# The activations of the feed-forward networks move into the work buffer, and the down weights by 160 bytes

## What is computed

```python
D_FF = -(-8 * D_MODEL // (3 * 256)) * 256        # 2816
def swiglu(x, w_gate, w_up, w_down):
    return (jax.nn.silu(x @ w_gate) * (x @ w_up)) @ w_down
```

## The kernel before

| tile | used as | byte in the partition | modulo 512 |
|---|---|---|---|
| `uT_h`, `uT_l` | moving (and weights in the output projections) | 32896, 41088 | 128 |
| `ring_r` | weights or moving | 63104 | 128 |
| `in_h` | weights | 49280 | 128 |
| `h_r` | weights of `down` | 112256 (over `ffb`) | 128 |
| `w_gu` | weights of `gate_up` | 138336 (start of `wk`) | 96 |
| `w_dn` | moving in `down` | 171136 | 128 |
| `out_h` (three) | moving in the output projections | 191584, 207968, 179296 | 96 |
| `fox_sum` (two), `fox_head` | moving and weights of a small product | 173152, 174176, 172128 | 96 |
| `odd_small` (two) | weights, 8 columns | 61568, 61824 | 128, 384 |

## Time and profile before

### The profile page before, as it was taken

The page is one execution under the profiler, slowest core; times in us unless marked ns, Lnnn a source line. Parts: engine busy times, 40 slices in busy tenths (PEclk is TensorE's granted clock), DMA queues, the critical chain, the costliest instruction groups (busy, mean ns, idle before and its releaser), DMA issues. The chain is left out here.

```text
span 1417.8 us, 25483 instructions
## 1 busy us (share of the span) xinstructions
PE 1390.4 (98%) x10044; PEld 1285.9 (91%) x10044; DVE 944.7 (67%) x1539; ACT 690.6 (49%) x1107; POOL 83.1 (6%) x137
## 2 busy tenths in 40 slices
PE   8999999999999999999999999999999999999997
PEld 8898888999989999899989999999998988899997
DVE  5768567666668666567567666676665676676665
ACT  6764546443354443376654443444443656643342
POOL 1030010000020000000000000100000123000000
PEclk9999999999999999999999999999999999999999
DMA  9344006655536554423356555365545423464540
GB/s 360 136 161 186 2 16 237 221 180 180 194 116 223 207 193 178 179 100 132 126 198 226 199 178 181 131 228 197 197 178 179 149 90 135 178 223 179 194 160 30
DMA packets 33069, 239.47 MB, mean 169 GB/s; under 512 B 6864, under 2 KB 13280, under 8 KB 14304
## 3 DMA queue, kind: packets, MB, share of 16 engines
q1 hardware_dynamic: 30320, 234.84, 45.6%
q10 hardware_dynamic: 2672, 3.58, 0.7%
HBM read 236.15 MB, written 2.25 MB: 168 GB/s over the span
## 5 line engine op out<-in xcount | busy, mean ns | idle before, releaser
L498 PE MATMUL ps<-uT_h,w_gu 128*128 128x256 f32 x3520 | 614.1, 280 | 2.6 <-ACT uT_h L1316 2.6
L498 PEld LDWEIGHTS ps<-uT_h,w_gu 128*128 128x128 f32 x3520 | 537.5, 188 | 13.4 <-issue 5.2
L498 PE MATMUL ps<-uT_l,w_gu 128*128 128x256 f32 x1760 | 478.9, 279 | 0.0
L498 PEld LDWEIGHTS ps<-uT_l,w_gu 128*128 128x128 f32 x1760 | 325.5, 188 | 0.0
L498 PE MATMUL ps<-w_dn,h_r 128*128 128x512 f32 x1320 | 320.9, 392 | 0.3 <-DVE h_r L2070 0.3
L1368 ACT CAST w_gu<-ring 128x2048 fp32r<-128x2048 f32 x110 | 209.8, 1908 | 153.5 <-PE ps L498 152.7
L498 PEld LDWEIGHTS ps<-w_dn,h_r 128*128 128x128 f32 x1320 | 239.7, 188 | 47.3 <-issue 1.5
L2028 DVE TENSOR_TENSOR w_gu<-ring,w_gu 128x2048 fp32r<-128x2048 f32 x110 | 252.1, 2292 | 35.2 <-ACT w_gu L1368 35.2
L2061 DVE TENSOR_TENSOR us<-ps,bc 128x256 f32<-128x256 f32 x110 | 46.5, 423 | 200.1 <-PE ps L498 200.1
L1381 ACT ACTIVATE wk<-wk 128x256 f32<-128x256 f32 x110 | 46.0, 418 | 263.8 <-DVE wk L2059 263.8
L1374 ACT CAST w_dn<-ring 128x1024 fp32r<-128x1024 f32 x110 | 115.6, 1051 | 78.4 <-PE ps L498 78.3
(11 more groups left out here) (398 smaller groups left out, 1696.1 us busy)
## 6 DMA issues: line engine op xcount, KB each, us to landing
ring<-wstream SPq DMA_DIRECT2D x144, 1536.0 KB, 6.5
cst<-consts_in SPq DMA_DIRECT2D x1, 2185.0 KB, 13.7
wk<-t_row ACTq DMA_DIRECT2D x1, 2048.0 KB, 7.8
wk<-masks_in SPq DMA_DIRECT2D x1, 1216.0 KB, 23.9
x<-x_in SPq DMA_DIRECT2D x2, 512.0 KB, 4.8
ring<-wstream SPq DMA_DIRECT2D x1, 1024.0 KB, 9.0
inh<-gains ACTq DMA_DIRECT2D x2, 512.0 KB, 9.7
tri_blocks<-wk SPq DMA_DIRECT2D x3, 256.0 KB, 2.8
```

What stands on the lines that cost most here:

```text
L498: return pe.matmul(o, l, r, start=start, stop=stop, skip_group_check=True)
```

## The change

The tile `h_r` no longer lies over `ffb`. It lies in the work buffer `wk`, right behind `w_dn`. `w_dn` starts 40 floats (160 bytes) later, and the gate results `sg` follow behind the new place of `h_r`.

```diff
-        w_dn = over("w_dn", [P, 2, 2, D], "wk", 8 * D + 8)
-        h_r = over("h_r", [P, 2, 2, T], "ffb")
+        w_dn = over("w_dn", [P, 2, 2, D], "wk", 8 * D + 48)
+        h_r = over("h_r", [P, 2, 2, T], "wk", 12 * D + 48)
...
-        sg = wk[:, 12 * D + 8:12 * D + 8 + 2 * T].rearrange("p (a b) -> p a b", a=2)
+        sg = wk[:, 13 * D + 48:13 * D + 48 + 2 * T].rearrange("p (a b) -> p a b", a=2)
```

## The result

The changed kernel takes 1425.35 us (median of 6 runs, 1424.87 to 1426.12), the one before 1420.21 us (6 runs, 1419.88 to 1420.95). The ratio is 1.0037, 95% interval 1.0027 to 1.0048: slower by 5.1 us, where 4.4 us less was forecast. The time is the one that the rival "the moving read gets dearer" gave, but the trace shows another mechanism.

What follows compares the result with a forecast made beforehand. PE was taken to bound the kernel. From 1419.59 us, down's matmuls gave -4.4 and gate_up, DVE and ACT, and order 0, so 1415.2 us; forecast's own range 1409 to 1417, 8-in-10 range 1409 to 1425.6.

Steps and rivals of the forecast that it cites:

- the moving read gets dearer: Rival: down's moving read at 288 costs 4.4 ns more per matmul, +5.8 us, 1425.4 us; chance 0.28.
- What bounds the kernel: PE, busy 98% of the span at 2.4 GHz and in all of the 8.36 us step; only its spending moves time.
- Step 1: Down's 1320 matmuls, both operands moved from 128 to 288 modulo 512: -3.3 ns each, -4.4 us.
- The bounds: Limits for down's matmuls: -15.8 us if weight reads cost nothing, +5.8 us at the dear neighbour's 234.4 ns.
- Step 2: Gate_up's matmuls, operands unmoved: cost taken as 0, with 1.1 us either way for the seams.
- the seams: Where gate_up and down meet in each step, first weights loading beside the other's last matmul; 1.1 us either way.
- Step 3: DVE and ACT work on the moved tiles: at most 0.2 us a step, hidden by over 6 us; cost 0.
- Step 4: Order and waits: all five programs keep the same waits, no queue passed, no transfer starts earlier; cost 0.
- only the difference counts: Rival: down's reads collide by their distance, 0 modulo 512 before and after; same pattern, no change, 1419.6 us; chance 0.30.
- What would show it: Trace checks: gate_up 5.60 us, down about 2.72; down 2.76 means the difference rule, 2.81 or more the dear moving read.
- The rule of the two independent read ports: Skill text against the whole change: weight loads take no read bandwidth from the running matmul, so placement is worth nothing.

Runs made afterwards that it cites:

- e6: Kernel before, but each network has its own equal remainder for w_dn and h_r (96, 160, 192, 224, 256 modulo 512), w_gu at 96; 1421.12 us.
- e1: Kernel before with h_r moved into the work buffer behind w_dn, both still at 128 modulo 512; 1420.2 us against 1420.2, ratio 1.000.
- e2: Kernel before with h_r moved into the work buffer at 288 modulo 512, w_dn left at 128; 1427.37 us, ratio 1.0049.
- e3: Kernel before with w_dn alone moved to 288 modulo 512, h_r left in its own tile at 128; 1427.53 us, ratio 1.0056.
- e4: Changed kernel plus one 64-column matmul, its result overwritten, ahead of each gate_up but a network's first; no address changed; 1432.87 us in one run.
- e13: e9 plus one 64-column matmul, its result overwritten, ahead of each gate_up but a network's first; no address changed; 1420.94 us.
- e7: Code of e6 with w_dn and h_r at 128; w_gu at 128 in networks 1 and 2, 160 in 3 and 4, 192 in 5; 1430.55 us.
- e9: Code of e6 with w_gu at 192 in all networks; w_dn and h_r as equal pairs at 96, 160, 192, 224, 256; 1416.32 us beside 1419.65 before.
- e10: As e9, with the equal pairs of w_dn and h_r at 288, 320, 352, 416, 480; 1415.66 us beside 1419.65 before.
- e11: Code of e6 with all pairs at 160; w_gu at 64 in networks 1 and 2, 256 in 3 and 4, 320 in 5; 1427.91 us.
- e12: Kernel before with w_gu at 192, w_dn and h_r at 224 modulo 512 in all networks, h_r in the work buffer; 1405.13 us against 1420.12, ratio 0.9895.

## Why the prediction was wrong

- **What bounds the kernel**: right. PE is busy in all of every step, and a change of a few ns per matmul arrives in full. The clock stayed at 2.4 GHz.
- **Step 1, down's matmuls, -4.4 us**: wrong. Down went from 2755 to 2758 ns a step, 110 x 3 ns = +0.3 us. The saving of 3.3 ns was carried over from a case in which only the weights had moved, so that the operands had become unequal; the change kept them equal. The row that belonged to the question was the settled 226.7 ns itself, which both-at-128 shows and which e6 finds again at five other places. That the sum stayed so near is in part luck: a longer beginning (+12 ns) and a cheaper hand-over (-9 ns) nearly cancel. The bounds (-15.8 and +5.8 us for this term) held the value.
- **Step 2, gate_up, "I take 0", with 1.1 us either way for the seams**: this is the step that failed and that carries the result. The seams themselves stayed within the bound: the hand-over to down rose by 9 ns (113 to 122) and the one back fell by 9 (235 to 226), about 1 us each way. But what goes ahead also decides in which rhythm the 48 matmuls run, and there the other 47 spacings rose by 49 ns together. For gate_up as a whole the term measured +5.13 us over the 95 steps that were compared, where 0 was forecast and 1.1 us allowed. The trace of before had shown the sign of it, a beginning of five matmuls that settles, and in its second network a gate_up at 117.8 ns; I read the first as a matter of down alone, and the second stands in none of my rows.
- **Step 3, DVE and ACT**: right. The copy and the subtraction into `h_r` stayed at 0.29 and 0.42 us, and PE still had over 6 us of cover. The timeline of DVE in the changed kernel:

```profile
306.94 0.29 DVE L2068 CAST h_r<-wk 128x256 fp32r<-128x256 f32 x1
307.27 0.42 DVE L2070 TENSOR_TENSOR h_r<-wk,h_r 128x256 fp32r<-128x256 f32 x1
```

- **Step 4, order and waits**: right; e1, with h in the new buffer and the same program, is at before's time.
- **The rival "only the difference counts"** was right on down's sum and its settled 226.7 ns, not on an unchanged pattern (eight dear spacings in place of five), and wrong on the time, since it left gate_up out. It lies nearest to what step 1 measured.
- **The rival "the moving read gets dearer"** gave 1425.4 us, which is what was measured, by a mechanism that did not occur: it asked for down at 2.81 us, and down is at 2.76. A time that fits is no proof of its reason; the fit is luck. In e2 and e3 down did get dearer by 40 to 53 ns a step, but in e2 the moving operand had stayed at 128, so it is the inequality and not the start of the moving read. The measured time also lies inside the range of 1409 to 1425.6 us, which is luck as well: the top of the range was there for this rival.
- **What would show it**: the text said that gate_up other than 5.60 us would mean that the seam, or something taken as untouched, moves too. That is what happened, and e2, e3, e4 and e13 show more of it: the rhythm changes at fixed addresses.
- **The rule of the two independent read ports** ("TensorE: Matmul & The Clock Gate", Step-by-step, in the Trainium skill), read as "placement is worth nothing", is not borne out for float32r: with the moving tile in one place gate_up takes 5.45 to 5.77 us, by the place of the weights and by the entry. No run shows whether the read ports are where that comes from.

What stays open: which part of the chip makes the rhythm. That DVE or ACT set it is unlikely, though not excluded by a run: in gate_up's 5.65 us they work for 3.29 and 1.47 us, while the spacings are the same from end to end. The runs show that it depends on remainders and on the entry, not why 192 with 224 lets the 113.3 ns hold. Of places finer than 32 bytes, and of other places of `uT`, nothing was run.

## What to carry to other kernels

Where float32r matmuls with a weight load each run back to back, read their spacings to the ns before pricing a move: a repeating pattern of three or four values, or a beginning that settles, is a sign that a change at one group can shift the group behind it. Price such a change over all matmuls of the repeating step, not only over those whose operands moved. Placement is cheap to sweep: give every repetition of a stage its own offsets, and one run compares five.

## What the runs showed of the hardware that was not expected

- The same 48 matmuls at the same addresses run at 5.60 or 5.65 us (e3), depending on how they are entered, and keep it for the rest of the network. In e7 they ran at 5.51 us once and at 5.65 from then on.
- Remainders modulo 256 bytes, not 512, seem to count: pairs at 96 and 352, 160 and 416, 224 and 480 gave the same gate_up, down and step to the ns (e9, e10), and so did `w_gu` at 64 and 320 (e11). `w_gu` at 0 and at 256 gave 5769 and 5690 ns, but beside different pairs (128 and 160), so they don't test it.
- Equal remainders of weights and moving operand were cheaper with 512 columns than the one unequal choice tried (2718 to 2783 ns for twelve over all equal pairs, against 2795 to 2808), and among the dearest with 256 (`w_gu` at 128: 5753 ns for 48, against 5598 at 96).
- Settled steps last a whole number of 6.67 ns, 16 cycles at 2.4 GHz: 8213, 8220, 8260, 8333, 8347, 8353, 8373, 8413, 8433 ns are 1232, 1233, 1239, 1250, 1252, 1253, 1256, 1262 and 1265 times that, rounded to the ns (as means over 15 steps, 8353.3, 8413.3 and 8213.3 ns before, after and in e12), and so are the settled steps of the other runs. This suggests a fixed beat behind the rhythms; no run isolates it.
- An added matmul made a step shorter (8.43 to 8.33, 8.37 to 8.31 and 8.37 to 8.28 us in networks 2, 3 and 5 of e9 and e13).
